# Query weights resident before the expert gather, a ring of five separate places, and the first head routed in two halves

## What is computed

```python
def rmsnorm(x, g):
    return x * rsqrt(mean(x * x) + 1e-6) * g

for l in range(2):
    h = rmsnorm(x, norm1_g[l])
    ...                                              # attention, state space, two gates
    x = x + (g_att * a_out + g_ssm * m_out) @ w_out[l]
    x = x + peer_ffn(rmsnorm(x, norm2_g[l]), ...)

def peer_ffn(h, wq, keys, u_tab, v_tab):             # 8 heads, 128 keys on each side, top 16
    qry = (h @ wq).reshape(b, s, 8, 2, 128)
    sc = einsum('bshcd,hckd->bshck', qry, keys)
    v1, i1 = top_k(sc[..., 0, :], 16)
    v2, i2 = top_k(sc[..., 1, :], 16)
    cand = v1[..., :, None] + v2[..., None, :]       # 16 x 16
    best, pos = top_k(cand, 16)
    idx = (i1 * 128 + i2) taken at pos
    gate = softmax(best)
    act = gelu(sum(u_tab[idx] * h))                  # one dot for each expert
    return sum(act * gate * v_tab[idx])
```

## Time and profile before

| what | value |
|---|---|
| median of 3 runs | 2359.17 us (2358.14 to 2359.28) |
| the profiled execution's own time | 2360.61 us |
| its span in the trace | 2357.8 us |
| PE busy | 2055.4 us (87%) |
| DVE busy | 1347.5 us (57%) |
| ACT busy | 758.7 us (32%) |
| POOL busy | 565.6 us (24%) |
| share of the chain that ended last: PE, DMA, DVE | 53%, 32%, 7% |
| granted PE clock in 40 slices, tenths | 9 in all but slice 26, which has 8 |
| GB/s in slices 10 to 19 of 40 (530 to 1120 us) | 420 to 423 each |
| gathers, 512 in all | 1 MB each, software queue, 554.87 MB with what else that queue moves |

### The profile page before, as it was taken

The page is one execution under the profiler, slowest core; times in us unless marked ns, Lnnn a source line. Parts: engine busy times, 40 slices in busy tenths (PEclk is TensorE's granted clock), DMA queues, the critical chain, the costliest instruction groups (busy, mean ns, idle before and its releaser), DMA issues.

```text
span 2357.8 us, 23073 instructions
## 1 busy us (share of the span) xinstructions
PE 2055.4 (87%) x8224; PEld 1312.6 (56%) x8224; DVE 1347.5 (57%) x3260; ACT 758.7 (32%) x2029; POOL 565.6 (24%) x598
## 2 busy tenths in 40 slices
PE   7999999999888787777789999999998888777775
PEld 6688888864444332222276888888644444322222
DVE  2367268148765576574423762781486765766644
ACT  2143257023333233323221432560233333233232
POOL 1000002014333333333210000020143333343331
PEclk9999999999999999999989999999999999999999
DMA  5423444559999999999723334445699999999996
GB/s 192 147 108 143 171 168 163 205 230 421 421 423 420 421 422 421 421 421 422 329 81 143 122 129 171 170 161 205 258 422 421 421 422 421 422 421 421 422 421 258
DMA packets 91426, 706.28 MB, mean 300 GB/s; under 512 B 10769, under 2 KB 10897, under 8 KB 16817
## 3 DMA queue, kind: packets, MB, share of 16 engines
q0 software_dynamic: 79424, 554.87, 57.1%
q1 hardware_dynamic: 11168, 146.29, 16.2%
q10 hardware_dynamic: 720, 3.67, 0.5%
HBM read 702.56 MB, written 1.18 MB: 298 GB/s over the span
## 4 chain that ended last, share of the span: by engine, by line
PE 53%; DMA 32%; DVE 7%; ACT 3%; issue 2%; POOL 2%; DVEq 0%; POOLq 0%; SPq 0%; ACTq 0%
DMA ring<-in_peer_uv,ex_i 31%; PE bank L424 23%; PE bank L693 10%; PE bank L409 7%; DVE ring L1379 5%; PE bank L634 3%; PE bank L600 2%; PE bank L445 2%; POOL ring L1489 2%; PE bank L581 2%; ACT diag L934 1%; ACT wgt L927 1%; PE bank L493 1%; PE bank L545 1%; PE bank L467 1%
## 5 line engine op out<-in xcount | busy, mean ns | idle before, releaser
L693 PE MATMUL bank<-ring,diag 128*128 128x512 f32 x2048 | 952.2, 609 | 253.2 <-ACT diag L934 252.7
L1379 DVE SCALAR_TENSOR_TENSOR ring<-ring,h 128x1024 f32<-128x1024 f32 x512 | 607.1, 1223 | 460.9 <-DMA ring<-in_peer_uv,ex_i 457.1
L693 PEld LDWEIGHTS bank<-ring,diag 128*128 128x128 f32 x2048 | 373.8, 192 | 795.8 <-ACT diag L934 416.5
L1489 POOL DMA_INDIRECT ring<-in_peer_uv,ex_i x512 | 501.8, 980 | 975.9 <-PE bank L693 680.0
L424 PE MATMUL bank<-hT,w_ring 128*128 128x256 f32 x2560 | 570.2, 383 | 1.9 <-ACT hT L724 1.9
L424 PEld LDWEIGHTS bank<-hT,w_ring 128*128 128x128 f32 x2560 | 485.4, 191 | 74.7 <-issue 7.4
L921 ACT ACTIVATE gel<-act_u 128x2 f32<-128x2 f32 x256 | 52.1, 203 | 862.2 <-DVE ring L1379 861.9
L934 ACT ACTIVATE diag<-cst,wgt 128x128 f32<-128x128 f32 x512 | 177.5, 394 | 8.4
L927 ACT ACTIVATE wgt<-gel,gate_w 128x1 f32<-128x1 f32 x512 | 123.0, 287 | 9.5
L1101 DVE SCALAR_TENSOR_TENSOR c_tmp<-xbc,par_all,c_tmp 128x254 f32<-128x254 f32 (+1 forms) x256 | 112.4, 480 | 4.5
L409 PE MATMUL bank<-zT,w_ring 128*128 128x256 f32 x512 | 111.0, 379 | 0.2
(11 more groups left out here) (196 smaller groups left out, 1703.8 us busy)
## 6 DMA issues: line engine op xcount, KB each, us to landing
w_ring<-in_w_stream SPq DMA_DIRECT2D x62, 2048.0 KB
fbuf<-cs_rows_dram POOLq DMA_DIRECT2D x32, 512.0 KB, 5.0
wq<-in_w_stream SPq DMA_DIRECT2D x4, 2048.0 KB, 10.1
ring<-in_peer_uv,ex_i POOLq DMA_INDIRECT x512
out<-in_w_stream SPq DMA_DIRECT2D x2, 2048.0 KB, 12.8
keys<-in_keys_t ACTq DMA_DIRECT2D x2, 1024.0 KB, 4.9
x_tok<-in_x SPq DMA_DIRECT2D x1, 1024.0 KB, 4.9
partner<-qk POOLq DMA_DIRECT2D x32, 32.0 KB, 7.0
```

The source lines that it names most:

```text
L693: ins = pe.matmul(bank[b0 + n][:], diag[:, PAIR * (m % 2) + s, :], ring[:, slot, DM + n * 512:DM + (n + 1) * 512], start=False, stop=True, ...
L1379: ins = dve.scalar_tensor_tensor(out=row, in0=row, scalar=1.0, in1=h2[:, b, :], op0=ALU.mult, op1=ALU.mult, accum_out=act_u[:, b, PAIR * k ...
L1489: pool.indirect_dma_start(ring[:, PAIR * q + s, :], None, peer_uv, bass.IndirectOffsetOnAxis(ap=ex_i[:, b, j:j + 1], axis=0))\
```

## The change

- The ring becomes five separate places (`ring_a`, `ring_c`, `ring_d`, `ring_f` and slot 0 of `w_ring`), taken in the order a, w, d, f, c. Pair 0 has a free place; pair 1 takes the slot of the first half of `w_out` and waits for `out_product(1, 0)` (`mix_full` 11); pair 2 takes the place of `out1`, pair 3 that of the gates, both after `mix_full` 12; pair 4 takes the place of `wq0`, as before.
- `wq2` and `wq3` get places of their own. SP loads `out1` one chunk of the state-space projection earlier, `wq0` and `wq3` beside its last two chunks, `wq(1)` and `wq2` when `out_product(0, 0)` begins.
- Since `w_ring`'s slot 0 is now a place of the ring, chunk 0 of layer 1, and chunk 1 behind it on SP, wait until the last pair of layer 0 has been used.
- `route(0)` becomes `first_eight` and `other_eight`: the eight best of a head come from the eight best of each side, so the first needs one round of max and index and 8 x 8 candidates. POOL starts on them (`first_experts`) and waits for the rest at pair 4. `other_eight` runs between the additions of block 1.
- PE: `out_product(1, 0)` and `(1, 1)` are finished before `query_tiles(2, 0)`; `turn_block(1)` and `query_tiles(0, 1)` come before the third chunk's queries, of which two tiles stand ahead of the pairs and two behind pairs 0 and 1. The late queries of heads 4 and 5 go behind pairs 2 to 8 (they were behind 0 to 6). ACT takes `squares(2)` and `gate_exp(0)` ahead of `query_out(2, 0)`.

```diff
-LATE = [(8, 0, 0), (12, 0, 12), (4, 1, 24), (8, 1, 36), (12, 1, 50)]
+LATE = [(4, 0, (-1, -1, 0, 1), 1, 1, 2), (8, 0, (2, 4, 6, 8), 8, 9, 11), (12, 0, (12, 14, 16, 18), 20, 21, 23),
+        (4, 1, (24, 26, 28, 30), 32, 33, 35), (8, 1, (36, 38, 40, 42), 44, 45, 47), (12, 1, (50, 52, 54, 56), 58, 59, 61)]
...
-        ring, at = place(at, "ring", [P, RING, 2 * DM])
-        out1, _ = place(arena + 6 * 2 * DM * 4, "out1", [P, 4096])
-        wq0, _ = place(arena + 8 * 2 * DM * 4, "wq0", [P, 4096])
+        pair_a, at = place(at, "ring_a", [P, PAIR, 2 * DM])
         wq3, at = place(at, "wq3", [P, 4096])
+        pair_c, _ = place(at, "ring_c", [P, PAIR, 2 * DM])
+        wq0, at = place(at, "wq0", [P, 4096])
+        pair_d, _ = place(at, "ring_d", [P, PAIR, 2 * DM])
+        out1, at = place(at, "out1", [P, 4096])
+        wq2, at = place(at, "wq2", [P, 4096])
+        pair_f, at = place(at, "ring_f", [P, PAIR, 2 * DM])
+        pair_w = w_ring[:, 0, :].rearrange("p (s n) -> p s n", s=PAIR)
+        ring = [pair_a, pair_w, pair_d, pair_f, pair_c]
...
+                    if L > 0 and c == 0:
+                        sync.wait_ge(pair_used.sem, pair_used.at(L - 1, LAYER_PAIRS - 1))
...
-                sync.wait_ge(mix_full.sem, mix_full.at(L, 12))
-                sync.dma_start(wq3[:], w_stream[CHUNKS * L + C_WQ + 3]).then_inc(wq3_loaded.sem, 16)
+                    if c == C_SSM + 2:
+                        sync.dma_start(wq0[:], w_stream[CHUNKS * L + C_WQ]).then_inc(wq0_loaded.sem, 16)
+                    if c == C_SSM + 3:
+                        sync.dma_start(wq3[:], w_stream[CHUNKS * L + C_WQ + 3]).then_inc(wq3_loaded.sem, 16)
+                sync.wait_ge(mix_full.sem, mix_full.at(L, 8))
+                sync.dma_start(wq2[:], w_stream[CHUNKS * L + C_WQ + 2]).then_inc(wq2_loaded.sem, 16)
...
                 key_scores(0, 0)
+                out_product(1, 0, range(7, 8))
+                out_product(1, 1, range(KD))
                 query_tiles(2, 0, range(2))
-                out_product(1, 0, range(7, 8))
                 key_scores(2, 0)
-                out_product(1, 1, range(KD))
-                chunk_wait(C_OUT + 1)
-                query_tiles(4, 0, range(4))
                 turn_block(1)
-                key_scores(4, 0)
-                chunk_wait(C_OUT + 2)
                 wait(bank_empty, FILL["t", 1, 1] + 1, L)
                 query_tiles(0, 1, range(4))
+                chunk_wait(C_OUT + 1)
+                pe.wait_ge(wq2_loaded.sem, wq2_loaded.at(L, 16))
                 key_scores(0, 1)
+                query_tiles(4, 0, range(2))
...
+                act.wait_ge(mix_empty.sem, mix_empty.at(L, 12))
+                squares(2, L, 1, 2)
+                gate_exp(0)
                 query_out(2, 0)
                 scores_out(2, 0)
-                gate_exp(0)
-                act.wait_ge(mix_empty.sem, mix_empty.at(L, 12))
-                squares(2, L, 1, 2)
-                query_out(4, 0)
                 turned(1)
-                scores_out(4, 0)
+                query_out(0, 1)
+                scores_out(0, 1)
...
+                def first_eight():
...
+                    for t in range(2):
+                        ins = dve.max(vals[:, t, n], sc[:, 0, t, :])
+                    step(ins)
+                    for t in range(2):
+                        dve.max_index(idxs[:, t, n], vals[:, t, n], sc[:, 0, t, :])
+                    flat = cand[:, 1].rearrange("p i j -> p (i j)")[:, 0:half * half]
+                    step(dve.tensor_tensor(flat.rearrange("p (i j) -> p i j", j=half), bc(vals[:, 0, n], 2, half),
+                                           bc(vals[:, 1, n], 1, half), ALU.add))
+                    step(dve.max(best[:, 0, n], flat))
+                    step(dve.max_index(posn[:, 0, n], best[:, 0, n], flat))
...
+                    e = eq[:, :, n, n]
+                    step(dve.tensor_tensor(e, bc(ab_f[:, :, n], 3, half), bc(bc(const("iota")[:, n], 1, half), 1, 2),
+                                           ALU.is_equal))
+                    step(dve.tensor_tensor(e, e, bc(idxf[:, 0:2, n], 2, half), ALU.mult))
+                    step(dve.tensor_reduce(selv[:, :, n], e, AX.X, ALU.add))
...
-                for _ in route(0):
-                    pass
-                add_and_norm(1)
+                first_eight()
+                add_half(1, 0)
+                others = other_eight()
+                next(others)
+                add_half(1, 1)
+                next(others, None)
+                norm(1)
                 softmax(0)
...
-                        if m == 3:
+                        if m == TOPK // 2 // PAIR:
+                            pool.wait_ge(experts_ready.sem, experts_ready.at(L, 1))
+                        if m == 1:
+                            pool.wait_ge(mix_full.sem, mix_full.at(L, 11))
+                        if m == 2:
                             pool.wait_ge(mix_full.sem, mix_full.at(L, 12))
```

More of the change, by code:

```diff
@@ L262, in encoder_kernel @@
         wq0_loaded = sem("wq0_loaded", 16)
+        wq2_loaded = sem("wq2_loaded", 16)
         wq3_loaded = sem("wq3_loaded", 16)
@@ L623, in wq @@
                 def wq(c):
-                    return wq0[:] if c == 0 else wq3[:] if c == 3 else w_ring[:, ring_slot(C_OUT + c), :]
+                    return (wq0[:], w_ring[:, ring_slot(C_OUT + 1), :], wq2[:], wq3[:])[c]
                 def query_tiles(t0, b, js):
@@ L1248, in _, with add_half, norm @@
                     wait(mix_empty, 4 + i + 1, L)
[L1250 to L1256 removed]
+                def add_half(b, c):
+                    n = 8 + 2 * b + c + 1
+                    dve.wait_ge(mix_full.sem, mix_full.at(L, n))
+                    xs = x_tok[:, b, c * 512:(c + 1) * 512]
+                    dve.tensor_tensor(xs, bank[4 + 2 * b + c][:], xs, ALU.add).then_inc(mix_empty.sem, 1)
+                def norm(b):
                     root(1 + b, b, b + 1)
@@ L1261, in add_and_norm @@
                                              op0=ALU.mult, op1=ALU.mult).then_inc(xn_ready.sem, 1)
-                add_and_norm(0)
+                add_half(0, 0)
+                add_half(0, 1)
+                norm(0)
                 def route(p):
@@ new lines, in other_eight @@
+                def other_eight():
+                    half = TOPK // 2
+                    n = slice(half, TOPK)
+                    for t in range(2):
+                        ins = dve.match_replace(sc[:, 0, t, :], vals[:, t, 0:half], sc[:, 0, t, :], NEG)
+                    step(ins)
+                    for t in range(2):
+                        ins = dve.max(vals[:, t, n], sc[:, 0, t, :])
+                    step(ins)
+                    for t in range(2):
+                        dve.max_index(idxs[:, t, n], vals[:, t, n], sc[:, 0, t, :])
+                    step(dve.tensor_tensor(cand[:, 0], bc(vals[:, 0, :], 2, TOPK), bc(vals[:, 1, :], 1, TOPK), ALU.add))
+                    flat = cand[:, 0].rearrange("p i j -> p (i j)")
+                    step(dve.match_replace(flat, best[:, 0, 0:half], flat, NEG))
+                    step(dve.max(best[:, 0, n], flat))
+                    g = gate_w[:, 0, 0:1, :]
+                    dve.tensor_tensor(g, best[:, 0:1], best[:, 0:1, 0:1].broadcast_to([P, 1, TOPK]),
+                                      ALU.subtract).then_inc(best_shift.sem, 1)
+                    yield
+                    step(dve.max_index(posn[:, 0, n], best[:, 0, n], flat))
+                    dve.tensor_scalar(ab_u[:, 0, n], posn[:, 0, n], 4, None, ALU.logical_shift_right)
+                    dve.tensor_scalar(ab_u[:, 1, n], posn[:, 0, n], 15, None, ALU.bitwise_and)
+                    step(dve.tensor_copy(idxf[:, 0:2, :], idxs[:, 0:2, :]))
+                    step(dve.tensor_copy(ab_f[:, :, n], ab_u[:, :, n]))
+                    e = eq[:, :, n, :]
+                    step(dve.tensor_tensor(e, bc(ab_f[:, :, n], 3, TOPK), bc(bc(const("iota"), 1, half), 1, 2),
+                                           ALU.is_equal))
+                    step(dve.tensor_tensor(e, e, bc(idxf[:, 0:2, :], 2, half), ALU.mult))
+                    step(dve.tensor_reduce(selv[:, :, n], e, AX.X, ALU.add))
+                    step(dve.scalar_tensor_tensor(out=selv[:, 0, n], in0=selv[:, 0, n], scalar=float(PK),
+                                                  in1=selv[:, 1, n], op0=ALU.mult, op1=ALU.add))
+                    dve.tensor_scalar(ex_i[:, 0, n], selv[:, 0, n], param("row0"), None, ALU.add)\
+                        .then_inc(experts_ready.sem, 1)
```

65 lines of the change are left out of this document (34 added, 31 removed).

## The result

| kernel | median | runs | ratio to before, 95% interval |
|---|---|---|---|
| before | 2359.23 us | 4, 2358.14 to 2360.20 | |
| after | 2345.78 us | 4, 2342.23 to 2347.92 | 0.9945 [0.9933, 0.9957] |
| after, measured again later | 2352.35 us | 11, 2350.33 to 2358.23 | 0.9984 [0.9975, 0.9993] |

The changed kernel is faster, by 0.6% in the first measurement and by 0.2% in the second. I forecast 2340 us and a range of 2330 to 2351: the first measurement lies in the range, 5.8 us above the forecast, and the second just outside it. The kernel before gave 2358.0 to 2359.2 in every measurement. So there are two questions: where 6 of the 19.4 us went, and why the changed kernel has no single time. The profile shown first is that of the first measurement: 2345.26 us, span 2343.0, which is 14.8 us less span than before.

What follows compares the result with a forecast made beforehand. The DMA engines bound the gather's steady part, and what POOL waits for before issuing bounds its beginning. Layer gains of 4.3 and 5.0 plus 10.1 for the next layer's loads make 19.4 us: 2340 us, range 2330 to 2351.

Steps and rivals of the forecast that it cites:

- the hole: DMA engines run dry behind the first pairs, 5.7 us before pair 5 and 2.8 us before pair 7.
- Chunks 0 and 1: Layer 1's first two weight chunks leave layer 0's gather, saving 10.1 us once, their loading covered by turning and norm.
- My 1179 among the signs: Expected sign in the profile after: no load on SP between 490 and 1179.
- its cover: Between layers, turning and norm hide chunk 0's load; without them it costs 8 us once.
- The projection beside which the other loads now stand: `wq0`, `wq3` and `out1` load beside projection chunks of 13.9 us each; hidden, PE's possible wait of 0 to 2 taken as 0.
- First gather: Start of layer 0's gather: shortened routing of head 0 saves 5.8 us, so it goes out at 505.2 instead of 511.05.
- PE's chain: PE's work up to pair 0: a new 3 us wait from 512, pair 0 at 532.0, pair 5 issued at 535.9.
- a pair with nothing ahead: Latency of a pair issued to an empty DMA queue: 7.4 us, range 5.0 to 8.2, from plain SP loads.
- Rival 1: PE's clock falls at its new wait near 512, lengthening work before pair 0 in both layers; 2345 us, chance 0.15.
- Rival 4: Slower: TensorE's half clock holds from 515 to pair 4, 16 us more in each layer; 2371 us, chance 0.04.

Runs made afterwards that it cites:

- alone: The kernel before with one wait added, so SP loads layer 1's chunks 0 and 1 only after pair 126 of layer 0 is used; 2351.27 us.
- the kernel before with two tiles: The kernel before with two query tiles, 3.6 us on PE, computed additionally ahead of pair 0 in each layer; 2366.59 us.
- the two with the tiles moved behind: Changed kernel with the query tiles ahead of pair 0 put behind pairs 0 and 1, later ones moved too: 2351.76 us; with VectorE's norm also earlier: 2353.52 us.
- the kernel with the sum early: Changed kernel with the four matmuls that begin block 0's sum moved into PE's wait between query tiles (2, 0) and their key scores; 2347.82 us.
- the kernel with head 0 in one piece: Changed kernel with head 0 routed in one piece again, so the first gather goes out later; 2347.77 us.
- both edited kernels before: The kernel before with chunks 0 and 1 held until pair 126 is used, 2351.27 us; and with two extra query tiles ahead of pair 0, 2366.59 us.
- norm first: Changed kernel with VectorE's norm of block 1 ahead of head 0's second routing half and ScalarE's gate exponential after its copies; 2347.53 us.

## Why the prediction was right, and where it was off

That 2345.78 lies between 2330 and 2351 is in part luck. One term of the sum was too small, which cost 4.4 us (the hole, below), and the profiled execution had no fall of the clock in front of pair 0, while the same kernel later gave 2352.35. What was right is the mechanism: two loads worth two pairs, a start bound by PE's way to pair 0, and DMA engines that run dry behind it.

**Chunks 0 and 1.** Forecast 10.1, measured 9.7 in the changed kernel and 8.2 alone. Chunk 0 was issued 2.8 us behind the dots of pair 127 (1162.35 and 1159.52), where I had 7.8 (1180 and 1172.21): the wait is for pair 126, which last used the slot, not for the last of all. My 1179 among the signs was a time of the kernel before and should have been some 14 us less. The step from pair 127's dots to line 438 stayed 19.1 us, so its cover holds. The projection beside which the other loads now stand takes 55.49 us in both kernels, so they are hidden, as I took it.

**First gather.** Forecast 505.2, measured 504.70, of which 0.5 is that everything ahead of it ran that much earlier. This step is right.

**PE's chain.** Forecast: idle from 512 to 515, pair 4 at 525.3, pair 0 on PE at 532.0, pair 5 issued at 535.9. Measured: idle 2.48 us to 513.88, 524.36, 530.62, 534.49. It is right within 1.4 us, and on the good side.

**The hole.** This is the step that failed, in one term: "a pair with nothing ahead needs 5.0 + 2.4 = 7.4". From issue to landing of the pair, the trace has 9.8 us for pair 5 (534.49 to 544.3), 9.6 for pair 7 (547.21 to 556.8) and 9.7 for pair 8 (552.93 to 562.6). The list of DMA issues with the time to landing, asked for one gather at a time, gives for the two of pair 5, the two of pair 7 and the two of pair 8:

```profile
ring_a<-in_peer_uv,ex_i POOLq DMA_INDIRECT x1, 6.2
ring_a<-in_peer_uv,ex_i POOLq DMA_INDIRECT x1, 7.8
ring_d<-in_peer_uv,ex_i POOLq DMA_INDIRECT x1, 6.6
ring_d<-in_peer_uv,ex_i POOLq DMA_INDIRECT x1, 7.5
ring_f<-in_peer_uv,ex_i POOLq DMA_INDIRECT x1, 7.2
ring_f<-in_peer_uv,ex_i POOLq DMA_INDIRECT x1, 8.3
```

Pair 5's first gather went out when the DMA engines had nothing to do, and its 1 MB took 6.2 us, not the 4.9 of a plain 1 MB load from SP that I went by. POOL sends the second one 2.03 us behind the first (1.72 or 1.76 and 0.30), where in a running sequence it is 1.24 (0.94 and 0.30), and the second gathers took 7.8 and 7.5. So 2.03 + 7.8 for pair 5, and 2.06 + 7.5 for pair 7. That is 2.2 to 2.4 more than 7.4. In layer 1 pairs 5, 7 and 8 took 9.4, 9.8 and 10.4. The upper end that I gave for this latency, 8.2, was too low as well; a plain load was the nearest row and the wrong kind. (The 9.0 for a pair with nothing ahead, in the expectation for the kernel before with two tiles, is too low: it takes 7.0, the median of pair 5's two gathers, for the second.)

Pair 8 shows what this costs. It was issued 48.2 us behind the first gather in both layers, where I had 48.7, and landed 9.7 and 10.4 us later instead of 7.4. The difference is 1.8 us in layer 0 and 2.5 in layer 1, together the 4.4 that are missing. The holes themselves are nearly as large as forecast: the windows from 532 to 552 hold 5.1 MB, where 421 GB/s would be 8.4, so 7.8 us are missing there (an estimate), and I had 5.7 + 2.8.

The mechanism behind that step is borne out by what doesn't vary. From pair 5's issue to pair 127's dots, nine profiles of the changed kind, two layers each, take 624.6 to 626.0 us, all but the two with the tiles moved behind. Their whole times stand 646.9 to 648.3 us behind pair 5's issue in layer 1: 1697.0 gives 2343.9, 1697.8 gives 2345.3, 1703.4 gives 2350.3, 1705.0 gives 2352.4, 1710.7 gives 2357.9.

**Rival 1** (the clock falls at PE's new wait; 2345 us, 0.15) was not what made the first profile 2345: the clock is 1.00 there from 508 to 576 and from 1672 to 1736. But it is a true cost of this kernel, in some executions: of the nine profiles, eight show 0.50 in front of pair 0 in at least one layer, twelve of eighteen layers in all. I had priced it at 2.5 us a layer; where it reaches into the query group, that group alone takes 1.6 to 2.7 more. The other three runs of the first measurement have no profile, so whether they had it isn't known. I had treated it as one case or the other, and it is a draw in each execution. The rule I quoted from the Trainium skill's "TensorE: Matmul & The Clock Gate", section "Why this matters for your kernels", no gap over about 3 us, fits in kind but not in the number: waits of 2.48 and 0.74 us kept the clock twice, 2.31 and 1.48 kept it, and even 3.47 and 0.74 kept it, while one of 2.28 lost it (before the 1.32 that followed), one of 2.06 lost it, and so did one of 2.65 after unbroken work. Rival 4's lasting half clock didn't come: the longest spell in front of pair 0 is some 10 us.

**What stays open.** ScalarE's late copy costs up to 2.6 us a layer by itself. Between executions whose ScalarE does the same up to there it is 0, or 1.1 to 2.6 us, and no engine's work of which I found a record ends then. It makes PE's wait longer, but that it starts the spell isn't shown: it came without one in layer 1 of the kernel with the sum early, and the kernel with head 0 in one piece has the spell in both layers without it. Whether the chip or the gather's traffic sets it wasn't tested, so why the first measurement's four runs were all below the second's eleven isn't settled either. Nor do these two make up all of the spread: from pair 127's dots to layer 1's first gather, the profiles of the changed kind with head 0 in two halves take 505.3 to 508.5 us.

## What to carry to other kernels

Once a queue is allowed to run dry, its latency is paid in full, with the issuing engine's own time in it: take it from a row of the same kind of DMA, issued after a pause, and ask for one DMA at a time, since a list gives medians. Winning time at the first issue is worth little when the ring's next free place hangs on a chain on another engine: find the one event from which all later time is a constant (here pair 5's issue) and count only what moves that. And this kernel, with TensorE in waits of 2 to 5 us on its critical path, has a distribution and not a time: profile such a kernel more than once, compare it with its variants in one group of runs, and move useful work into the wait.

## What the hardware showed that I had not expected

- One program, two profiles: 2345.3 and 2350.3 us, medians 6.6 us apart, while the kernel before stayed within 1.2 us in all four comparisons.
- ScalarE can stand 1.1 to 2.8 us before a copy with only "remote" as its releaser, while PE's last matmul for it ended 1.7 to 4.6 us earlier. It is so in nine of the eleven profiles of the changed kind, in this place, while the first gathers land, and at ScalarE's first copy behind the norm in both edited kernels before.
- PE's granted clock fell after a wait of 2.28 us and stayed after 2.31 and 1.48 us in the other layer of the same execution (norm first), and it fell after 2.06 us and stayed after 3.47 in the two layers of another (sum early), so a wait's length alone doesn't tell.
- POOL's first indirect gather after a pause of 5 us or more took 1.2 to 1.8 us in most profiles, but 0.94 in others after pauses just as long (8.34 us in that of before), so the pause alone doesn't set it.
